# Attention of two heads at a time, and the order around retention, in layers 1 and 2 of a three-layer network

## What is computed

```python
def hybrid_layer(x, ...):
    h = rms_norm(x, g_mix_pre)
    u = h @ w_in
    aq, ak, av, cu, rq, rk, rv, rg = jnp.split(u, SPLITS, axis=-1)
    y_att = chunk_attention(aq, ak, av, rel_bias)      # 6 heads of 64
    y_conv = conv_module(cu, ...)
    y_ret = retention(rq, rk, rv, rg)                   # 6 heads of 64
    mix = jnp.concatenate([y_att, y_conv, y_ret], axis=-1) @ w_out
    x = x + rms_norm(mix, g_mix_post)
    ...                                                 # feed-forward part

# attention, per head: softmax(q k^T / 8 + bias, masked) v
# retention, per head: ((q k^T) * decay) v with rotary q and k,
# then layer norm per head and a gate silu(g)
```

## Time and profile before

| | us |
|---|---|
| median of 3 runs | 2670.1 (2669.8 to 2672.3) |
| profiled execution | 2669.7 |
| its span, first to last instruction | 2667.9 |
| TensorE matmul busy | 2583.3 |
| DVE busy | 1325.6 |
| ScalarE busy | 943.3 |
| GpSimd busy | 416.7 |
| span of slots 0 to 20, layer 1 / layer 2 | 94.66 / 94.62 |
| span from slot 21 to the first product of w_out, layer 1 / layer 2 | 41.72 / 42.36 |

### The profile page before, as it was taken

The page is one execution under the profiler, slowest core; times in us unless marked ns, Lnnn a source line. Parts: engine busy times, 40 slices in busy tenths (PEclk is TensorE's granted clock), DMA queues, the critical chain, the costliest instruction groups (busy, mean ns, idle before and its releaser), DMA issues.

```text
span 2667.9 us, 30576 instructions
## 1 busy us (share of the span) xinstructions
PE 2583.3 (97%) x11800; PEld 2033.4 (76%) x11800; DVE 1325.6 (50%) x1675; ACT 943.3 (35%) x1326; POOL 416.7 (16%) x365
## 2 busy tenths in 40 slices
PE   8998999999999999999999999999999989999998
PEld 6865788887876678888788888777776667888886
DVE  6754542333865453243443342589974447433332
ACT  4333542323333443232332232444344454322221
POOL 2101100001110100000111100268720320111101
PEclk9999999999999999999999999999999999999999
DMA  4310222232220122222222222411231033222222
GB/s 152 135 35 32 79 95 97 93 109 95 87 104 32 51 79 107 95 95 95 79 95 99 101 91 103 165 68 64 95 111 64 17 142 111 95 95 99 90 92 80
DMA packets 40712, 241.72 MB, mean 91 GB/s; under 512 B 4768, under 2 KB 5280, under 8 KB 17440
## 3 DMA queue, kind: packets, MB, share of 16 engines
q1 hardware_dynamic: 39472, 232.95, 24.6%
q0 software_dynamic: 560, 5.24, 0.5%
q10 hardware_dynamic: 576, 2.10, 0.2%
HBM read 231.88 MB, written 8.39 MB: 90 GB/s over the span
## 4 chain that ended last, share of the span: by engine, by line
PE 90%; DVE 4%; ACT 3%; issue 2%; DMA 0%; POOL 0%; DVEq 0%; SPq 0%; ACTq 0%; POOLq 0%
PE gemm L431 73%; PE gemm L612 2%; PE gemm L613 2%; PE gemm L621 2%; PE score L785 1%; PE mixed L806 1%; ACT w_hi L369 1%; PE score L1631 1%; DVE w_lo L378 1%; PE mixed L1642 1%; PE score L1689 1%; PE turned L796 1%; PE gemm L1748 1%; PE turned L1703 1%; PE gemm L459 0%
## 5 line engine op out<-in xcount | busy, mean ns | idle before, releaser
L378 DVE TENSOR_TENSOR w_lo<-w_raw,w_hi 128x2048 fp32r<-128x2048 f32 (+2 forms) x219 | 469.5, 2144 | 637.5 <-ACT w_hi L369 637.3
L431 PE MATMUL gemm<-h_hi,w_hi 128*128 128x512 f32 x1776 | 706.7, 398 | 3.1 <-DVE w_lo L378 2.6
L431 PE MATMUL gemm<-h_hi,w_lo 128*128 128x512 f32 x1776 | 693.7, 391 | 0.0
L431 PE MATMUL gemm<-h_lo,w_hi 128*128 128x512 f32 x1776 | 693.0, 390 | 0.0
L369 ACT ACTIVATE w_hi<-w_raw 128x2048 fp32r<-128x2048 f32 (+2 forms) x219 | 385.4, 1760 | 420.7 <-PE gemm L431 372.8
L431 PEld LDWEIGHTS gemm<-h_hi,w_hi 128*128 128x128 f32 x1776 | 334.4, 188 | 75.4 <-issue 4.9
L431 PEld LDWEIGHTS gemm<-h_hi,w_lo 128*128 128x128 f32 x1776 | 334.2, 188 | 71.0
L431 PEld LDWEIGHTS gemm<-h_lo,w_hi 128*128 128x128 f32 x1776 | 334.6, 188 | 67.2 <-issue 1.7
L431 PE MATMUL gemm<-f_hi,w_hi 128*128 128x512 f32 x512 | 199.2, 389 | 0.0
L431 PE MATMUL gemm<-f_lo,w_hi 128*128 128x512 f32 x512 | 199.2, 389 | 0.0
L431 PE MATMUL gemm<-f_hi,w_lo 128*128 128x512 f32 x512 | 199.2, 389 | 0.0
(11 more groups left out here) (391 smaller groups left out, 3695.4 us busy)
## 6 DMA issues: line engine op xcount, KB each, us to landing
w_raw<-in_w SPq DMA_DIRECT2D x173, 1024.0 KB, 4.7
w_raw<-in_w SPq DMA_DIRECT2D x16, 768.0 KB, 4.0
w_raw<-in_w SPq DMA_DIRECT2D x16, 640.0 KB, 3.7
w_raw<-in_w SPq DMA_DIRECT2D x14, 512.0 KB, 3.4
bias_t<-in_att_bias SPq DMA_DIRECT2D x2, 1536.0 KB, 8.7
decay_t<-in_c_decay SPq DMA_DIRECT2D x2, 1536.0 KB, 8.2
x_sb<-in_x SPq DMA_DIRECT2D x4, 512.0 KB, 6.3
x_kept<-x_sb SPq DMA_DIRECT2D x1, 2048.0 KB, 12.2
```

Source lines behind the costliest of these rows:

```text
L378: dve.tensor_tensor(w_lo[:, b.slot, 0:size], w_raw[:, b.slot, 0:size], w_hi[:, b.slot, 0:size].bitcast(F32), ALU.subtract).then_inc(S["w_r ...
L431: mm = pe.matmul(dst, lhs, rhs, start=b.first and k == 0 and j == 0, stop=b.last and k == b.kt - 1 and j == 2)
```

## The change

Attention's steps are ordered by pairs of heads: head 0 and head 1 for block 0, then both for block 1, and so on. In every even slot TensorE issues the scores of steps i and i + 1, one in each half of the rows, then mix_two(i - 4), which forms the mixes of two heads block by block by turns in the two halves of the columns, and then turn(i - 2). Odd slots hold the swaps and turn(i - 2) only. In ScalarE's queue the exponential comes after the copy of the transposed step and after the copy of o_ps, from step 23 on. The two buffers of decayed scores change places. In retention two more steps of scores and mixes come ahead of the last two steps of attention. ScalarE copies the bank of pair 0 (pair_out(0)) before the gates' silu. On DVE the centring of pair 0 and the first splits come two steps later, the scaling of pair 1 and its centring too, and the rest of the first w_out weights is computed in two halves, one before that centring and one after the last decayed scores. The order of DVE's attend is unchanged (its operations are only put into functions; cut below).

```diff
@@ -297,7 +297,7 @@
         ret_sq_last = at("ret_sq_last", [P, SEQ], F32, FZ + 60.5)
 
         sc_off = [0, 512, 896, 1152]
-        ret_sc_p = [at("ret_sc_even", [P, 2, 1280], F32, FZ), at("ret_sc_odd", [P, 2, 1280], F32, FZ + 50.5)]
+        ret_sc_p = [at("ret_sc_even", [P, 2, 1280], F32, FZ + 50.5), at("ret_sc_odd", [P, 2, 1280], F32, FZ)]
 
         def ret_sc(h, j):
             return ret_sc_p[h // 2 % 2][:, h % 2, sc_off[j]:sc_off[j] + SEQ - P * j]
@@ -377,6 +377,15 @@
             size = b.kt * b.w
             dve.tensor_tensor(w_lo[:, b.slot, 0:size], w_raw[:, b.slot, 0:size],
                               w_hi[:, b.slot, 0:size].bitcast(F32), ALU.subtract).then_inc(S["w_rest"], 1)
+
+        def rest_columns(dve, n, part):
+
+
+            b = plan[n]
+            dve.wait_ge(S["w_rounded"], n + 1)
+            c = slice(part * b.kt * b.w // 2, (part + 1) * b.kt * b.w // 2)
+            dve.tensor_tensor(w_lo[:, b.slot, c], w_raw[:, b.slot, c], w_hi[:, b.slot, c].bitcast(F32),
+                              ALU.subtract).then_inc(S["w_rest"] if part else S["half_rest"], 1)
 
         def half_of(buf, b, m):
             return view(buf, b)[:, :, m * P:(m + 1) * P]
@@ -652,7 +661,7 @@
         SOFT_AT = 8
         ROTARY_AT = 10
 
-        att_steps = [(h, q) for h in range(ATT_HEADS) for q in range(TOKT)]
+        att_steps = [(2 * p + e, q) for p in range(ATT_HEADS // 2) for q in range(TOKT) for e in range(2)]
         N_ATT = len(att_steps)
 
         def slots_of(b):
@@ -661,7 +670,7 @@
 
         slot0 = {b.i: sum(slots_of(c) for c in plan[SOFT_AT:b.i]) for b in plan[SOFT_AT:N_IN]}
         N_SLOT = sum(slots_of(c) for c in plan[SOFT_AT:N_IN])
-        rot_at = {slot0[ROTARY_AT] + 2 * j: j for j in range(6)}
+        rot_at = {slot0[ROTARY_AT] + 2 * j + 1: j for j in range(6)}
 
         def ring_of_score(s):
 
@@ -669,7 +678,7 @@
 
         def ring_of_swap(j):
 
-            i = slot0[ROTARY_AT] + 2 * j
+            i = slot0[ROTARY_AT] + 2 * j + 1
             return ring_of_score(min(i, N_ATT - 1)) + 1
 
         N_RING = N_ATT + 6
@@ -796,31 +805,35 @@
                     mm = pe.transpose(t_ps[:, P * j:P * j + P], probs[:, s % 4, P * j:P * j + P], ident[:])
                 mm.then_inc(S["turned_ps"], 1)
 
-            def mix(s):
+            def mix_two(s):
+
+
                 h, q = att_steps[s]
-                pe.wait_ge(S["turned"], cnt("turned", s + 1))
-                if q == 0 and h % 2 == 0 and h:
+                pe.wait_ge(S["turned"], cnt("turned", s + 2))
+                if q == 0 and h:
                     pe.wait_ge(S["att_out"], cnt("att_out", h // 2))
-                r = slice(HD * (h % 2), HD * (h % 2) + HD)
                 for j in range(q + 1):
-                    mm = pe.matmul(o_ps[r, P * q:P * q + P], value(HD * h, j),
-                                   probs_t[:, s % 2, P * j:P * j + P], start=j == 0, stop=j == q)
-                mm.then_inc(S["mixed_ps"], 1)
+                    for e in range(2):
+                        mm = pe.matmul(o_ps[HD * e:HD * e + HD, P * q:P * q + P], value(HD * (h + e), j),
+                                       probs_t[:, (s + e) % 2, P * j:P * j + P], start=j == 0, stop=j == q)
+                        if j == q:
+                            mm.then_inc(S["mixed_ps"], 1)
 
             def attend(i):
 
                 if i == 0:
                     pe.wait_ge(S["g_free"], plan1[6].t0 + TOKT)
                     pe.wait_ge(S["pool_r"], cnt("pool_r", 6))
-                if i < N_ATT:
+                if i < N_ATT and i % 2 == 0:
                     scores(i)
+                    scores(i + 1)
                 if i in rot_at:
                     pe.wait_ge(S["pool_r"], cnt("pool_r", 7 + rot_at[i]))
                     swapped(rot_at[i])
+                if 4 <= i <= N_ATT + 2 and i % 2 == 0:
+                    mix_two(i - 4)
                 if 2 <= i <= N_ATT + 1:
                     turn(i - 2)
-                if 3 <= i <= N_ATT + 2:
-                    mix(i - 3)
 
             if lay == 0:
                 opening(pe, plan1[:2], N0, out_sb, 0, FIRST_OPENING, turned=lay)
@@ -894,11 +907,13 @@
             attend(N_SLOT + 2)
             two(ret_scores, 2)
             two(ret_mixed, 0)
-            attend(N_SLOT + 3)
             two(ret_scores, 4)
             two(ret_mixed, 2)
+            attend(N_SLOT + 3)
+            two(ret_scores, 6)
+            two(ret_mixed, 4)
             attend(N_SLOT + 4)
-            for s in range(6, N_RET + 2, 2):
+            for s in range(8, N_RET + 2, 2):
                 if s < N_RET:
                     two(ret_scores, s)
                 two(ret_mixed, s - 2)
@@ -1024,14 +1039,18 @@
                 else:
                     act.activation(dst, tile_of(b, m), ACT.Copy, scale=inverse[:, m:m + 1]).then_inc(S["g_free"], 1)
 
-            def softmax(i):
-
+            def exponents(i):
                 if i < N_ATT:
                     q = att_steps[i][1]
                     act.wait_ge(S["maxed"], cnt("maxed", i + 1))
                     act.activation(probs[:, i % 4, 0:P * (q + 1)], probs[:, i % 4, 0:P * (q + 1)], ACT.Exp,
                                    bias=tiny[:, i % 4:i % 4 + 1],
                                    accum_out=tiny[:, 4 + i % 4:5 + i % 4]).then_inc(S["exped"], 1)
+
+            def softmax(i):
+
+                if i <= N_SLOT:
+                    exponents(i)
                 if 2 <= i <= N_ATT + 1:
                     p = i - 2
                     q = att_steps[p][1]
@@ -1044,6 +1063,8 @@
                     pair = (i - 2) // (2 * TOKT)
                     act.wait_ge(S["mixed_ps"], cnt("mixed_ps", 2 * TOKT * pair))
                     act.activation(out_sb[:, pair - 1, :], o_ps[:], ACT.Copy).then_inc(S["att_out"], 1)
+                if i > N_SLOT:
+                    exponents(i)
 
             round_block(act, plan1[1].n + 2)
             for m in range(2):
@@ -1083,6 +1104,11 @@
                 act.wait_ge(S["ln_done"], cnt("ln_done", q + 1))
                 act.activation(out_sb[:, 3 + q, :], out_sb[:, 3 + q, :], ACT.Silu, scale=ln_g[:, q:q + 1],
                                bias=ln_b[:, q:q + 1]).then_inc(S["act_own"], 1)
+            def pair_out(p):
+                act.wait_ge(S["ret_mix"], cnt("ret_mix", 2 * TOKT * (p + 1)))
+                act.activation(out_sb[:, 5 + p, :], ret_bank[p][:], ACT.Copy).then_inc(S["ret_out"], 1)
+
+            pair_out(0)
             act.wait_ge(S["pool_r"], cnt("pool_r", 15))
             for q in range(PAIRS):
                 act.activation(rg[:, q, :], rg[:, q, :], ACT.Silu).then_inc(S["rg_gate"], 1)
@@ -1095,8 +1121,8 @@
             act.wait_ge(S["act_own"], cnt("act_own", 2))
             act.wait_ge(S["att_out"], cnt("att_out", 3))
             for p in range(PAIRS):
-                act.wait_ge(S["ret_mix"], cnt("ret_mix", 2 * TOKT * (p + 1)))
-                act.activation(out_sb[:, 5 + p, :], ret_bank[p][:], ACT.Copy).then_inc(S["ret_out"], 1)
+                if p:
+                    pair_out(p)
                 if p < 2:
                     for k in ((0, 1), (2, 3, 4))[p]:
                         split_mixed(k)
...
@@ -1301,19 +1334,18 @@
                                          op1=ALU.mult).then_inc(S["ret_sc_s"], 1)
                 if s == 1:
                     attend(N_SLOT + 2)
-                if s == 11:
+                if s == 13:
                     centre(1)
-                if s == 13:
+                if s == 15:
                     rest_mixed(0)
-                if s == 15:
                     rest_mixed(1)
-                if s == 17:
+                if s == 19:
                     pair_scale(1)
-                if s == 19:
+                if s == 21:
+                    rest_columns(dve, plan1[W_OUT].n, 0)
                     centre(2)
-                if s == 21:
-                    rest_block(dve, plan1[W_OUT].n)
                 if s == 23:
+                    rest_columns(dve, plan1[W_OUT].n, 1)
                     rest_mixed(2)
                     rest_block(dve, plan1[W_OUT + 1].n)
             rest_mixed(3)
```

More of the change, by code:

```diff
@@ L1237, in attend, with inverted, scaled @@
                 p = i - 1
+                def inverted():
+                    dve.wait_ge(S["exped"], cnt("exped", i))
+                    dve.reciprocal(tiny[:, 8 + p % 4:9 + p % 4], tiny[:, 4 + p % 4:5 + p % 4]).then_inc(
+                        S["inverted"], 1)
+                def scaled():
+                    size = P * (att_steps[p][1] + 1)
+                    dve.wait_ge(S["inverted"], cnt("inverted", i))
+                    dve.tensor_scalar(probs[:, p % 4, 0:size], probs[:, p % 4, 0:size],
+                                      tiny[:, 8 + p % 4:9 + p % 4], None, ALU.mult).then_inc(S["scaled"], 1)
                 if i < N_ATT:
@@ L1249, in attend @@
                 if 1 <= i <= N_ATT:
-                    dve.wait_ge(S["exped"], cnt("exped", i))
```

(8 more changed lines are left out.)

## The result

The changed kernel takes 2606.5 us (2605.6 to 2607.1, 4 runs) against 2670.6 (2669.8 to 2672.3, 4 runs) for the kernel before: a ratio of 0.976, 95% interval 0.9744 to 0.9775. The direction and the parts were right; two of the parts were too small, because each left out a term.

The account below looks back on a forecast made before the run. TensorE's queue was taken to bound the slots, while the tail was two thirds work, the rest waits and slow clock. Savings of 24.0 us in layer 1 and 25.5 in layer 2, 49.5 together, gave 2621 us, range 2611 to 2637.

Parts of the forecast that it names:

- Do two heads run side by side?: Attention's scores and mixes: a pair of two heads costs what one costs, as retention's 1.06 us against 1.05.
- The slots: Slots 0 to 20 of each layer: 7.35 us saved on scores, 6.15 on mixes, 13.7 a layer in all.
- the transpositions are unchanged but for their order, 7.91 against 7.69: In the slots of each layer, transpositions cost 7.91 us before and 7.69 after, at 0.26 to 0.59 each.
- the changes of form are inside the prices: Slots and tail: start-to-start prices of scores, mixes and transpositions already hold the array's changes of form; no separate term.
- The wait at the token piece: At the start of that piece in the slots, TensorE's 1.2 us idle stays; bounds 0 and 2.4 a layer.
- The tail: From slot 21's score to the first w_out product: 10.3 us saved in layer 1, 10.9 in layer 2.
- the three places named: Tail waits that stay: behind the copies of steps 20 and 21, 0.35 and 0.65 us, and 0.4 at pair 0's variance.
- The paired work: TensorE's own work in the tail falls by 3.44 us a layer through paired scores and mixes.
- The clock's term: In the tail, the clock of 0.95 gives back 1.5 us a layer, bounds 0 and 2.1.
- The rivals: Four alternatives: tail keeps waits, 2636 us (0.09); mixes don't pair, 2637 (0.05); nothing pairs, 2655 (0.03); slower, 2676 (0.02).
- The tail did not keep its waits: Rival: new late copies or splits replace the tail's old waits, only 3.44 us of work goes; 2636 us, chance 0.09.
- no score waits for DVE's read of a swap: Slower rival: second scores wait for DVE's read of a swap, 2.5 us each even slot; 2676 us, chance 0.02.

Follow-up runs that it names:

- b_mixfirst: The kernel before with the mix issued ahead of the transposition in each slot instead of behind it; 2668.3 us, ratio 0.9987.
- a_turnfirst: The changed kernel with the transposition issued ahead of the paired mixes in the even slots; 2612.0 us.
- b_tail: The kernel before with only the changed kernel's reordering behind the slots, heads not paired and buffers not exchanged; 2650.3 us, ratio 0.9925.
- a_best: The changed kernel with three more edits: earlier copies from step 21 on, earlier scaling of pair 2, later rest of piece 11's weights; 2599.5 us.
- a_mix_seq: The changed kernel with each pair of mixes issued head after head instead of block by block by turns; 2612.0 us.

## Why the prediction was wrong

**Do two heads run side by side?** Right. Each of the paired groups costs what the forecast said, and undoing either pairing costs what its prices and the changes of form gave (20.9 for 19 to 22, and 16.9, just under the 17 to 21).

**The slots.** The step that failed is the sentence that the transpositions are unchanged but for their order, 7.91 against 7.69. The count was right and the price wrong. I had taken prices from start to start in a slot in which score, transposition, mix and dense product each use the array in another form (64 rows, full, 64 columns, full), so each price held one change of form. After the change the transposition always stands beside the dense product, and in the odd slots there is no score and no mix at all. The rows of after give 0.41 instead of 0.59, 0.25 instead of 0.48 and 0.08 instead of 0.26, about 0.2 us less each. Where the odd slots begin without a score, the dense product goes over into the transposition after 0.23 us (137.68 to 137.91) as if into one of its own kind. Added up from start to start over the slots of layer 1, in us:

| | before | after | saved | forecast |
|---|---|---|---|---|
| scores | 15.17 | 7.83 | 7.3 | 7.35 |
| mixes | 11.99 | 5.95 | 6.0 | 6.15 |
| 19 transpositions | 7.35 | 3.86 | 3.5 | 0.2 |
| swaps, dense product, the convolution's mean | 58.9 | 57.7 | 1.2 | 0 |

So scores and mixes were priced right, and what the forecast put at nothing are the changes of form at the transpositions and, smaller, ahead of the scores (a dense matmul is followed by a score after 0.21 or 0.32 us, by one of its kind after 0.12 or 0.23). TensorE's busy time fell by 18.4 us (18.1 when added up so), 4.7 more than 13.7; 0.6 of it went into new idle time. As a count: slots 0 to 20 had 78 changes of form (2 in each of slots 0 to 2, 4 in each of 18) and now have 31 (2 in slots 0 and 2, 3 in each of nine even slots, none in the odd ones). Of the 47 that went, 19 were inside the prices of the 10 scores and 9 mixes that I took out; of the other 28, 18 stood behind a transposition, at 0.15 to 0.2 us, and 10 ahead of a score, at 0.09. b_mixfirst and a_turnfirst show the first price, 0.15 and 0.20 us, by moving one transposition and nothing else. The clue stood in the trace of before, where a lone transposition ahead of a mix costs 0.26 for some 0.1 of work; I wrote that the changes of form are inside the prices, and did not ask how many of them stay. The Trainium skill says that a change of tiling mode drains TensorE (TensorEngine Tiling (Array Packing), Key Properties). The traces agree as far as they go: across a change of form no weight load is drawn ahead, and the place costs 0.09 to 0.2 us.

**The wait at the token piece** came as followed: 1.2 before, 1.4 after (1.18 + 0.23), within its bounds of 0 and 2.4. The place is another than I wrote: no second score waits for DVE's read of a swap; the swap of slot 9 waits (144.26) until DVE has read slot 8's score from its bank. A wait of 0.4 at slot 5 I had not followed; it is the same chain one piece earlier.

**The tail.** The idle time left was 1.35 us for a forecast of 1.5: 0.34, 0.58 and 0.16 at the three places named, and 0.28 at one that was not, the mixes behind step 19's copy. The paired work went as priced within 0.3. The clock's term, 1.5 with a bound of 2.1, measured 1.9 in layer 1. The step that failed is that a wait was counted as its idle time and slow clock alone: the late second product of a pair, 1.1 us a layer, stood nowhere in the sum. That the tail is "two thirds work" was misread too: 34.85 of 41.72 us are five sixths. Of the four reorderings DVE's order is worth 5.0 us a layer, pair 0's copy 3.5, the exponential's place 0.5 and the weave -0.2, which add up to the 8.8 of b_tail; the forecast had expected all four to matter. That sum mixes two kernels: the first four are measured with the heads paired, b_tail without.

**Elsewhere.** 2.8 us were saved where no instruction changed, 2.1 of them in the last stretch; the forecast had this at nothing. Over the profiles of the twelve experiments the last stretch takes 1760.2 to 1763.6 us with the same instructions, and the one of before 1762.9. By the traces' clock records it takes 1760.2 to 1760.9 us where TensorE spends 37 to 38 us of it at 1.2 GHz, and 1762.0 to 1763.6 where it spends 41 to 45; before has 44, after 38. One wait in layer 3 differs as well (6.3 us before, 4.4 after), but a_best has the 6.3 and takes 1760.9. Whether that can be steered stays open; for a forecast it is an uncertainty of 3 us that mine did not hold.

**The rivals.** None took place. The tail did not keep its waits, and in the trace no score waits for DVE's read of a swap.

## What to carry to other kernels

Price a small matmul by what stands before and behind it, and when a change moves matmuls, count the changes of the array's form as an item of their own: here some 0.1 to 0.2 us each, and 47 fewer in the slots of each layer. Put those of the full form next to the dense product, and those that use half of the rows or columns in pairs. When waits of an engine go, expect more back than its idle time: look at whether the clock is slow behind the wait and whether the second of a pair starts late. Test the reordering without the rest of the change: here it was worth 20 us by itself and could have been had alone.

## What the runs showed of the hardware

- Two fp32 products in the two column halves, with all rows in use, run side by side at the price of one (16 records in 1.03 us), in the same PSUM bank and while each accumulates.
- In a_mix_seq the second half comes up to two products (four records) behind in the queue and still runs beside the first; with three and four the group takes 1.08 and 1.51 us instead of 0.80 and 1.03.
- Moving one transposition from ahead of a mix to behind it saves 0.15 us, with the same matmuls (b_mixfirst).
- At a change between full, 64-row and 64-column form the next weight load starts only with its own matmul, 0.20 us or more after the start of the last one (138.75 and 139.77 in before); between kinds of the same form it starts with the last one (149.23 in after).
- Where DVE is late, the second product of a pair starts 0.33 to 0.46 us behind the first, and the profile counts this as busy time (231.89, 239.33 and 242.83 in before).
